# A hybrid decoder step on one core: sharing out the one-hots of the expert gates anew, and moving the early weights' low halves to GpSimd

## What is computed

```
idx = i_top[0] * 128 + i_top[1]            # 8 heads x 16 of a token
gates = softmax(best)
act = gelu(einsum('td,tkd->tk', x, expert_u[idx]))
out = einsum('tk,tkd->td', gates * act, expert_v[idx])
```

## Time and profile before

| | |
|---|---|
| median of 3 runs | 1886.55 us (1886.25 to 1886.7) |
| profiled execution, span | 1884.2 us; the profile gives no other time of this execution |
| TensorE busy | 1838.8 us, 98% |
| VectorE busy | 1540.2 us, 82% |
| ScalarE, GpSimd busy | 869.0 and 771.1 us |
| the 96 quads | from 777.7 to 1016.4 us |

### The profile page before, as it was taken

The page is one execution under the profiler, slowest core; times in us unless marked ns, Lnnn a source line. Parts: engine busy times, 40 slices in busy tenths (PEclk is TensorE's granted clock), DMA queues, the critical chain, the costliest instruction groups (busy, mean ns, idle before and its releaser), DMA issues.

```text
span 1884.2 us, 34734 instructions
## 1 busy us (share of the span) xinstructions
PE 1838.8 (98%) x13193; PEld 1670.2 (89%) x13193; DVE 1540.2 (82%) x3073; ACT 869.0 (46%) x1535; POOL 771.1 (41%) x572
## 2 busy tenths in 40 slices
PE   6999999999999999999999999999999999999998
PEld 3779999999877999999999888988888888888887
DVE  4577777777666889989795888989899899998998
ACT  3525455455343335688886434333343333333333
POOL 0000000000033434987783345555455565555662
PEclk9999999999999999999999999999999999999999
DMA  9732222222452426686777999999999999999984
GB/s 394 275 114 85 85 80 80 85 75 84 166 196 73 151 68 211 209 245 198 217 222 228 344 372 383 390 385 391 380 376 382 388 386 372 376 378 372 369 338 153
DMA packets 179732, 474.78 MB, mean 252 GB/s; under 512 B 16752, under 2 KB 79184, under 8 KB 176240
## 3 DMA queue, kind: packets, MB, share of 16 engines
q1 hardware_dynamic: 133488, 304.78, 46.2%
q0 software_dynamic: 46080, 167.79, 23.3%
HBM read 426.57 MB, written 45.94 MB: 251 GB/s over the span
## 4 chain that ended last, share of the span: by engine, by line
PE 54%; DVE 10%; DMA 2%; issue 1%; POOL 1%; ACT 0%; DVEq 0%; ACTq 0%
PE dd L2836 17%; PE pp L2823 16%; PE pp L2836 8%; PE pp L2440 7%; PE dd L2791 4%; DMA x<-in_v,idx 1%; POOL hot_a L2602 1%; DVE top_i L2483 1%; DVE top_i L2472 1%; DVE less L2473 1%; DVE top L3081 1%; DVE top_v L2478 1%; DVE top_v L2467 1%; PE pp L468 1%; DMA v_raw<-in_v 1%
## 5 line engine op out<-in xcount | busy, mean ns | idle before, releaser
L452 ACT ACTIVATE w_hi<-w_raw 128x1024 fp32r<-128x1024 f32 x202 | 212.8, 1054 | 146.3 <-PE pp L468 89.6
L456 DVE TENSOR_TENSOR w_lo<-w_raw,w_hi 128x1024 fp32r<-128x1024 f32 x176 | 216.1, 1228 | 33.4 <-ACT w_hi L452 33.3
L468 PE MATMUL pp<-act_hi,w_hi 128*128 128x272 f32 x1040 | 232.9, 305 | 2.3 <-DVE w_lo L456 0.7
L468 PE MATMUL pp<-act_hi,w_lo 128*128 128x272 f32 x1040 | 215.0, 288 | 0.0
L468 PE MATMUL pp<-act_lo,w_hi 128*128 128x272 f32 x1040 | 214.8, 288 | 0.0
L3018 ACT ACTIVATE co_hi<-cf 128x384 fp32r<-128x384 f32 x126 | 66.3, 526 | 320.6 <-PE pp L2836 256.9
L2823 PE MATMUL pp<-act_hi,w_hi 128*128 128x384 f32 x616 | 208.8, 339 | 0.0
L2823 PE MATMUL pp<-act_lo,w_hi 128*128 128x384 f32 x616 | 207.6, 337 | 0.0
L2602 POOL TENSOR_SCALAR hot_a<-cst,gcols 128x128 f32<-128x128 f32 x144 | 191.5, 1338 | 39.1 <-PE dd L2791 38.8
L2823 PE MATMUL pp<-act_hi,w_lo 128*128 128x384 f32 x616 | 207.1, 336 | 0.0
L3311 DVE TENSOR_TENSOR v_lo<-v_raw,v_hi 128x1024 fp32r<-128x1024 f32 x126 | 154.0, 1222 | 29.2 <-ACT v_hi L3006 27.8
(11 more groups left out here) (499 smaller groups left out, 4584.5 us busy)
## 6 DMA issues: line engine op xcount, KB each, us to landing
w_raw<-in_stream SPq DMA_DIRECT2D x206, 512.0 KB
v_raw<-in_v SPq DMA_DIRECT2D x128, 512.0 KB
ada_w<-in_ada SPq DMA_DIRECT2D x24, 1024.0 KB, 10.3
gt<-gate_matrix SPq DMA_DIRECT2D x31, 768.0 KB
gate_matrix<-gstage SPq DMA_DIRECT2D x11, 2048.0 KB, 10.1
early<-cst SPq DMA_DIRECT2D x50, 192.0 KB, 4.2
cst<-early SPq DMA_DIRECT2D x50, 192.0 KB
wrow<-in_wout SPq DMA_DIRECT2D x8, 512.0 KB, 7.6
```

The costliest lines, as they stand in the source:

```text
L452: nc.scalar.activation(w_hi[k.slot][:], w_raw[k.slot][:], ACT.Copy).then_inc(w_hi_done, 1)
L456: nc.vector.tensor_tensor(w_lo[k.slot][:], w_raw[k.slot][:], w_hi[k.slot][:].bitcast(F32), ALU.subtract).then_inc(w_lo_done, 1)
L468: last = nc.tensor.matmul(pp[s][:, b, 0:HN], w[:, c * P:(c + 1) * P], a[:, c, b * HN:(b + 1) * HN], start=(c == 0 and w is w_hi[s] and a i ...
```

## The change

All four hot_a of a quad are compared by VectorE in one wide operation too, into a new buffer `first_of`, and then scaled by the gate: two by GpSimd in one product, two by ScalarE in one copy each. Both now wait for `hots_vector`. `away`, the alternating shares and the negated gates go. The 36 low halves of the stage move from VectorE's to GpSimd's order, behind the product of the same quad as before; what is left of them is done by GpSimd at the end of the stage. VectorE waits once for them before it takes over again.

```diff
-        picks = at("picks", 57 * K, [P, 4, P])
-        gcols = [at(f"gcols{s}", (59 + 53 * s) * K, [P, 4, P]) for s in range(2)]
+        picks = at("picks", 57 * K, [P, 3, P])
+        gcols = [at(f"gcols{s}", (59 + 53 * s) * K, [P, 3, P]) for s in range(2)]
-        away = at("away", 70 * K, [P, 4, P])
+        first_of = at("first_of", 114 * K, [P, 4 * HOTS, P])
-
-        def shares(q):
-            return ((2, 1, 1), (1, 1, 2))[q % 2]
+        BY_POOL = 2
...
+                lows = [E_HEAD - 1]
+
+                def low(i):
+                    assert i == lows[0]
+                    early_low(pool, Chunk(C_EARLY + i + 2))
+                    lows[0] += 1
+
                 for u in range(ND):
-                    pool.wait_ge(gcols_ready, u + 1)
                     for q in range(TQ):
-                        pool.wait_ge(quad_done, u * TQ + (q + 1))
-                        for o in range(shares(q)[0]):
-                            c = 4 * q + o
-                            last = nc.gpsimd.tensor_scalar(hot_a[:, (q % HOTS) * 4 + o, :], iota,
-                                                           gcols[u % 2][:, 0, c:c + 1], gcols[u % 2][:, 2, c:c + 1],
-                                                           ALU.is_equal, ALU.mult)
-                        last.then_inc(hots_pool, 1)
+                        v, c = (q % HOTS) * 4, 4 * q
+                        pool.wait_ge(hots_vector, u * TQ + (q + 1))
+                        nc.gpsimd.tensor_tensor(hot_a[:, v:v + BY_POOL, :], first_of[:, v:v + BY_POOL, :],
+                                                gcols[u % 2][:, 2, c:c + BY_POOL].unsqueeze(2).to_broadcast([P, BY_POOL, P]),
+                                                ALU.mult).then_inc(hots_pool, 1)
                         if u == 0 and q == 1:
                             fetch(pool, RING - 1)
+                        if (u, q) == (0, 4):
+                            low(E_HEAD - 1)
+                        for i in E_AT.get(u * TQ + q - LOW_LAG, ()):
+                            low(i)
+                while lows[0] < NE:
+                    low(lows[0])
...
-                    for n in range(4):
+                    for n in range(3):
                         last = nc.tensor.transpose(pp[0][:, 1, n * P:(n + 1) * P], picks[:, n, :], ident)
...
-                        if q < TQ:
-                            own = range(4 * q + 4 - shares(q)[2], 4 * q + 4)
-                            act.wait_ge(gcols_ready, u + 1)
-                            act.wait_ge(quad_done, u * TQ + (q + 1))
-                            for n, c in enumerate(own):
-                                nc.scalar.activation(away[:, (aways[0] + n) % 4, :], iota, ACT.Abs,
-                                                     bias=gcols[u % 2][:, 0, c:c + 1], scale=-1.0).then_inc(away_done, 1)
...
                         if q < TQ:
-                            act.wait_ge(away_done, aways[0] + len(own))
-                            for n, c in enumerate(own):
-                                last = nc.scalar.activation(hot_a[:, (q % HOTS) * 4 + c % 4, :],
-                                                            away[:, (aways[0] + n) % 4, :], ACT.Relu,
-                                                            bias=gcols[u % 2][:, 2, c:c + 1],
-                                                            scale=gcols[u % 2][:, 3, c:c + 1])
+                            v = (q % HOTS) * 4
+                            act.wait_ge(hots_vector, u * TQ + (q + 1))
+                            for o in range(BY_POOL, 4):
+                                last = nc.scalar.activation(hot_a[:, v + o, :], first_of[:, v + o, :], ACT.Copy,
+                                                            scale=gcols[u % 2][:, 2, 4 * q + o:4 * q + o + 1])
                             last.then_inc(hots_scalar, 1)
-                            aways[0] += len(own)
...
                 def hot(u, q):
                     dve.wait_ge(quad_done, u * TQ + (q + 1))
                     v, c, g = (q % HOTS) * 4, 4 * q, gcols[u % 2]
-                    last = nc.vector.tensor_tensor(hot_b[:, v:v + 4, :], iota.unsqueeze(1).to_broadcast([P, 4, P]),
-                                                   g[:, 1, c:c + 4].unsqueeze(2).to_broadcast([P, 4, P]), ALU.is_equal)
-                    first = shares(q)[0]
-                    for o in range(first, first + shares(q)[1]):
-                        last = nc.vector.tensor_scalar(hot_a[:, v + o, :], iota, g[:, 0, c + o:c + o + 1],
-                                                       g[:, 2, c + o:c + o + 1], ALU.is_equal, ALU.mult)
+                    for to, n in ((first_of, 0), (hot_b, 1)):
+                        last = nc.vector.tensor_tensor(to[:, v:v + 4, :], iota.unsqueeze(1).to_broadcast([P, 4, P]),
+                                                       g[:, n, c:c + 4].unsqueeze(2).to_broadcast([P, 4, P]), ALU.is_equal)
                     last.then_inc(hots_vector, 1)
-
-                    if (u, q) == (0, 4):
-                        low(E_HEAD - 1)
-                    for i in E_AT.get(u * TQ + q - LOW_LAG, ()):
-                        low(i)
-
-                def low(i):
-                    assert i == lows[0]
-                    k = Chunk(C_EARLY + i + 2)
-                    dve.wait_ge(w_lo_done, k.n)
-                    split_lo(dve, k)
-                    lows[0] += 1
...
                     if b + 3 in J_OF and J_OF[b + 3] >= 2:
+                        if J_OF[b + 3] == 2:
+                            dve.wait_ge(w_lo_done, C_U + 2)
                         split_lo(dve, Chunk(C_U + J_OF[b + 3]))
```

More of the change, by code:

```diff
@@ L2489, in build @@
             sem("p5_dve"), sem("ex_in"), sem("ex_out"), sem("picks_ready"), sem("picks_tr"), sem("chosen"))
-        gcols_ready, hots_vector, hots_pool, hots_scalar, away_done, quad_done, quad_read = (
-            sem("gcols_ready"), sem("hots_vector"), sem("hots_pool"), sem("hots_scalar"), sem("away_done"),
-            sem("quad_done"), sem("quad_read"))
+        gcols_ready, hots_vector, hots_pool, hots_scalar, quad_done, quad_read = (
+            sem("gcols_ready"), sem("hots_vector"), sem("hots_pool"), sem("hots_scalar"), sem("quad_done"),
+            sem("quad_read"))
         gates_st = [sem(f"gates_st{s}") for s in range(2)]
@@ L2937, in _ @@
                         exponents(1)
-                aways = [0]
                 def beside_choice(u):
                     for q in range(TQ + 2):
-                        if q < TQ:
-                            own = range(4 * q + 4 - shares(q)[2], 4 * q + 4)
-                            act.wait_ge(gcols_ready, u + 1)
-                            act.wait_ge(quad_done, u * TQ + (q + 1))
-                            for n, c in enumerate(own):
-                                nc.scalar.activation(away[:, (aways[0] + n) % 4, :], iota, ACT.Abs,
-                                                     bias=gcols[u % 2][:, 0, c:c + 1], scale=-1.0).then_inc(away_done, 1)
                         if q >= 2:
@@ L3093, in take @@
                     dve.wait_ge(picks_tr, u + 1)
-                    nc.vector.tensor_copy(gcols[u % 2][:], pp[0][:, 1, :].rearrange("p (n t) -> p n t", n=4)).then_inc(
+                    nc.vector.tensor_copy(gcols[u % 2][:], pp[0][:, 1, 0:3 * P].rearrange("p (n t) -> p n t", n=3)).then_inc(
                         gcols_ready, 1)
                     dve.wait_ge(gcols_ready, u + 1)
-                lows = [E_HEAD - 1]
                 def hot(u, q):
@@ L3208, in choice @@
                     if t < ND:
[L3209 to L3212, removed]
                         nc.vector.tensor_tensor(picks[:, 2, :].rearrange("p (h k) -> p h k", h=H), best[:],
@@ L3239, in _ @@
                         take(u + 1)
-                while lows[0] < NE:
-                    low(lows[0])
                 st = Steps(dve, sp_dve)
```

## The result

The changed kernel takes 1938.07 us (median of 4 runs, 1937.21 to 1938.79) against 1886.55: 1.0267 times as long, 95% interval 1.0253 to 1.0282. That is 51.5 us more, where 32 were predicted, within the range of 1897 to 1946. The profiled execution spans 1935.5 us against 1884.2.

The account below looks back on a forecast made before the run. TensorE, busy for 98% of the span, was taken as the bound. Its waits for late low halves in three tiles, 33.7 us, less 1.8 us given back, made +31.9 us: 1918.5 us, range 1897 to 1946.

Parts of the forecast that it names:

- What bounds, what can be won: Whole kernel: TensorE busy for 98% of the span; its 2.72 us idle in the stage nearly all there was to win.
- Stops: Dense stretches: GpSimd stops VectorE's two-operand work, 2.07 us per low half, 0.5 per product; 1.7 and 0.4 counted there.
- one-operand work that I had counted as cover: Choice's small searches outside dense stretches have one operand: only 1.2 us counted per low half, nothing per product.
- The chain of 4.6 us: Per low half: two compares 1.28, hand-over 0.1, product 0.75, low half 2.40, 0.05 to TensorE; before, 2.1 us.
- rival b: Stops don't matter, only the longer chain: first tile's low half behind quad 7 3.7 us late; 1888.5 us, chance 0.09.
- the quarter of a 128x1024: GpSimd's 256-column product: at least 0.6 us, a quarter of the 2.40 for 128x1024; 0.75 was taken.
- TensorE's waits: Low half behind quad 21 of each tile late: TensorE loses 15.1, 9.8 and 8.8 us, sum 33.7.
- the sum: Whole kernel: 33.7 us of TensorE's waits less 1.8 gives +31.9 us, 1918.5 us.
- a lighter ScalarE: Stage: 192 scaled copies replace 141 pairs of Abs and Relu; 1.5 us of TensorE's idle time comes back, bounds 0 and 2.7.
- upper bound: Top of the range, 1946 us: stops of 2.1 us per low half and 1.0 per product, 59.4 us, nothing given back.
- (c): Stage gets faster: VectorE's lead grows, low halves are in time, ScalarE's lighter share closes holes; 1881 us, chance 0.04.
- (d): GpSimd becomes the bound of the whole stage, 3.4 us per quad against 2.49: +86 us, 1972 us, chance 0.07.

Follow-up runs that it names:

- e3: The changed kernel with the row of indices for VectorE's wide compares read from PSUM instead of SBUF, same order: 1906.59 us, ratio 1.0094.
- e6: The changed kernel with compare indices from PSUM and low halves three quads after their product's end instead of five: 1889.61 us, ratio 1.0008.
- e8: The original kernel with only the 36 low halves moved from VectorE to GpSimd: 1906.65 us, ratio 1.0099.
- e1: The changed kernel with the low halves given back to VectorE, all else as changed: 1918.77 us, ratio 1.0165.

## Why the prediction was right, and where its size was off

- **What bounds, what can be won.** Right: all other stages kept their times within 1 us, and no version went measurably below the original.
- **Stops.** Right in kind and size. I took 2.07 us per low half and 0.4 per product; the changed kernel's timeline shows 2.14 and 0.41. Undisturbed, these operations of GpSimd take 2.40 and 0.61 themselves. e3 shows the cause apart from all else: same order, same work, no stops of the compares, -31.5 us. They also hit one-operand work that I had counted as cover: a copy of 128x8 took 2.37 us beside a low half.

```profile
796.52 2.37 DVE L3120 COPY gsum<-best 128x8 f32<-128x8 f32 x1
```

```profile
795.28 3.59 POOL L2457 TENSOR_TENSOR w_lo<-w_raw,w_hi 128x1024 fp32r<-128x1024 f32 x1
```

  The Trainium skill (SBUF — State Buffer, "Who interferes with whom") says that VectorE's copy can enter a mode that takes the access shared with GpSimd. These rows agree; the same copy took 0.16 us in the original's timeline (at 793.41).
- **The chain of 4.6 us.** Right as a mechanism: e3, free of stops on the compares, keeps 13.6 us of waits for low halves, and a lag of 3 (e6) leaves 1.3. I had put this alone at 3.7 us (rival b); e3 has 13.6, in all three tiles. Probably the second compare takes part of VectorE's lead too; no run shows this by itself. One term was off: the product takes 0.61 us undisturbed, not 0.75, about the quarter of a 128x1024 that I had called the least.
- **TensorE's waits.** I summed 15.1 + 9.8 + 8.8 = 33.7 us. Measured: 36.3, in three groups of 12.0, 11.2 and 13.1 us (the timeline's 20 waits summed), each with one wait of 4.6 in the dense stretch. So the sum came out by luck in part: the first tile was put 3 us too high, the third 4 too low. And I had all of a tile's loss at the last low half of its dense stretch, where it came in six or seven waits, the first in the stage (3.55 us at 790.28) for the low half behind quad 4, where rival (b) had quad 7.
- **What was missing.** The step "the sum" took the waits as the whole cost. TensorE's matmuls themselves took 15.8 us more, as the granted clock fell to 0.95. That is most of the 19.5 us between 32 and 51.5; another 3 are idle time, 35.1 us more against the 31.9 of my sum, in which I had given back 1.5 for a lighter ScalarE. The range held the result only because its upper bound took every stop at its longest; no term of it stood for slower matmuls. That part is luck. ScalarE did get lighter (162 us busy for 197), but TensorE's waits for it in the stage went from 1.7 to 3.3 us, as its copies now wait for VectorE.
- **Rivals.** (b) is refuted by e3, (c) by every run. (d) is refuted: GpSimd is busy for 177 of 290 us; in e8, with other work, it is full and the cost is 19, not 86.

The clock's fall goes with TensorE's idle time over all the kernels of the table: at 2.6 to 5.5 us idle the clock is 0.99 to 1.00 and TensorE busy for 235.4 to 237.5; at 10.5 and 12.0, 0.99 and 239 and 242; at 14 to 15, 0.97 and 244 to 245; at 22.6 to 37.8, 0.95 to 0.96 and 248 to 252. Where the idle time is over 2 us above the original's, each microsecond of it came with 0.4 to 0.8 more in slower matmuls. What sets off a single fall stays open: it came behind waits of 4.59 and 1.77 us (818.00, 834.33), and not behind one of 2.62 (880.61).

Open, too, is why a product on GpSimd is starved in e1 at 909.30 and not in the changed kernel at 814.21, where it also arrives while VectorE runs a band operation, and gets its turn at the end of that.

## What to carry to other kernels

Work moved off a busy engine is not free if the two engines share access to their operands: look in the trace for a place where both already do such work, and read what each takes from the other; here one row pair gave the stop to within 0.1 us. Moving one operand to PSUM removed it for the compares, where moving work could not. Where TensorE is the bound, price its waits at more than their length, since here the matmuls behind some of them ran slower; and when a helper's operation moves to another engine's queue, count its whole chain anew and move its place in the order with it.

## What the hardware showed unexpectedly

- The hold-up goes both ways and is not fair: VectorE's compares were stopped for up to 2.2 us by one low half, and in e1 GpSimd's 0.61 us product lasted 8.62 and 9.75 us under VectorE's unbroken run of two-operand operations. The Trainium skill (SBUF — State Buffer, "Who interferes with whom") says that the later instruction waits until the end of the earlier one. For the stops the trace agrees to within 0.3 us (2.14 us by a low half of 2.40, 0.41 by a product of 0.61); for the product starved at 909.30 the measurement decides: it outlasted the eleven VectorE operations from 909.14 on.
- A VectorE compare with one operand in PSUM was not touched by GpSimd's two-operand work (at most 693 ns in 192 compares), and took no longer than with both in SBUF (690 and 681 ns at the median, 692 in the earlier trace rows).
- The low clock of TensorE made 0.32 us of 0.18 per matmul of 384 columns for 3 us behind a wait of 4.59 us.
